# Reordering the first W_up pieces on x1: the third pair's first piece between quarters two and three, the fourth pair in PSUM banks 4 and 5

## The reference, cut to what matters

```python
x = x + rmsnorm(mix, norm_post_mix)                       # x1
hid = jnp.square(jax.nn.relu(rmsnorm(x, norm_pre_mlp) @ w_up))
x = x + rmsnorm(hid @ w_down, norm_post_mlp)              # w_up 2048 x 8192, w_down 8192 x 2048
```

## Time and profile before

| | us |
|---|---|
| median of 3 runs | 1793.79 (1793.65 to 1793.89) |
| the profiled execution | 1794.34 |
| its span, first to last instruction | 1792.7 |
| PE busy | 1775.9 (99%) |
| DVE busy | 1089.4 (61%) |
| ACT busy | 763.9 (43%) |
| POOL busy | 449.3 (25%) |
| granted TensorE clock, mean | 0.999 |

### The profile page before, as it was taken

One profiled execution on the slowest core, in us unless ns is written; L12 is line 12 of the kernel. 1 busy time (PEld: TensorE's weight loads), 2 busy tenths in 40 slices (PEclk: granted clock), 3 DMA queues, 4 the chain that ended last, 5 costly groups with the idle time before them and its releaser, 6 DMA issues.

```text
span 1792.7 us, 34869 instructions
## 1 busy us (share of the span) xinstructions
PE 1775.9 (99%) x13199; PEld 1742.6 (97%) x13199; DVE 1089.4 (61%) x2004; ACT 763.9 (43%) x1116; POOL 449.3 (25%) x351
## 2 busy tenths in 40 slices
PE   8999999999999999999999999999999999999998
PEld 7999999999998989999899999999999999999998
DVE  5587878999778777865875333444344444444444
ACT  7443435555356565633543333333333332333442
POOL 1577776677651222223000000000000000000132
PEclk9999999999999999999999999999999999999999
DMA  8555554554545555554345444544444444454442
GB/s 253 190 177 159 154 155 134 153 153 143 156 150 167 161 181 161 190 192 141 118 145 161 141 152 146 161 152 141 151 138 160 155 147 142 140 158 155 155 142 83
DMA packets 287305, 278.42 MB, mean 155 GB/s; under 512 B 11590, under 2 KB 284718, under 8 KB 286336
## 3 DMA queue, kind: packets, MB, share of 16 engines
q1 hardware_dynamic: 249064, 247.87, 44.0%
q10 hardware_dynamic: 36496, 21.77, 4.1%
q0 software_dynamic: 1648, 7.43, 1.3%
HBM read 261.25 MB, written 17.22 MB: 155 GB/s over the span
## 4 chain that ended last, share of the span: by engine, by line
PE 96%; DVE 2%; ACT 1%; DMA 0%; issue 0%; SPq 0%; DVEq 0%; ACTq 0%
PE ps L1801 29%; PE ps L1803 29%; PE ps L1802 29%; PE ps L2095 1%; PE ps L2045 1%; PE ps L2068 1%; PE ps L2105 1%; PE ps L2139 1%; PE ps L1859 1%; PE ps L2141 1%; PE ps L2140 1%; PE ps L1860 1%; PE ps L1861 1%; DMA xn<-in_x_prompt 0%; DVE mix L1668 0%; DVE wlo L1198 0%
## 5 line engine op out<-in xcount | busy, mean ns | idle before, releaser
L1801 PE MATMUL ps<-ahi,whi 128*128 128x320 f32 x2304 | 717.9, 312 | 0.0
L1803 PE MATMUL ps<-ahi,wlo 128*128 128x320 f32 x2304 | 711.9, 309 | 0.0
L1802 PE MATMUL ps<-alo,whi 128*128 128x320 f32 x2304 | 711.9, 309 | 0.0
L681 ACT ACTIVATE whi<-raw 128x1024 fp32r<-128x1024 f32 x463 | 478.4, 1055 | 446.7 <-PE ps L1803 383.0
L1198 DVE TENSOR_TENSOR wlo<-raw,whi 128x1024 fp32r<-128x1024 f32 x344 | 424.3, 1257 | 236.6 <-ACT whi L681 233.7
L1801 PEld LDWEIGHTS ps<-ahi,whi 128*128 128x128 f32 x2304 | 432.5, 188 | 2.1 <-issue 0.5
L1802 PEld LDWEIGHTS ps<-alo,whi 128*128 128x128 f32 x2304 | 432.6, 188 | 0.5
L1803 PEld LDWEIGHTS ps<-ahi,wlo 128*128 128x128 f32 x2304 | 432.5, 188 | 0.0
L1801 PE MATMUL ps<-hhi,whi 128*128 128x320 f32 x1016 | 314.3, 309 | 0.0
L1803 PE MATMUL ps<-hhi,wlo 128*128 128x320 f32 x1016 | 313.9, 309 | 0.0
L1802 PE MATMUL ps<-hlo,whi 128*128 128x320 f32 x1016 | 313.9, 309 | 0.0
(11 more groups left out here) (324 smaller groups left out, 1603.6 us busy)
## 6 DMA issues: line engine op xcount, KB each, us to landing
raw<-in_w_in SPq DMA_DIRECT2D x144, 512.0 KB, 3.5
raw<-in_w_up SPq DMA_DIRECT2D x128, 512.0 KB, 4.2
raw<-in_w_down SPq DMA_DIRECT2D x128, 512.0 KB, 4.5
raw<-in_w_out SPq DMA_DIRECT2D x64, 512.0 KB, 3.7
h<-in_state_ssm ACTq DMA_DIRECT2D x16, 512.0 KB, 4.9
out<-hout ACTq DMA_DIRECT2D x16, 512.0 KB, 3.2
x_transposed<-xt ACTq DMA_DIRECT2D x1, 2560.0 KB, 13.5
xr<-x_transposed POOLq DMA_DIRECT2D x1, 2560.0 KB, 9.6
```

Source lines behind the costliest of these rows:

```text
L681: act.activation(whi[:, kq, :, 0:width], raw[:, kq, :, 0:width], ACT.Copy).then_inc(hi_done, 1)
L1801: pe.matmul(out, wh, hi[:, kk, :], start=(kk == 0), stop=False)
L1802: pe.matmul(out, wh, lo[:, kk, :], start=False, stop=False)
L1803: last = pe.matmul(out, wl, hi[:, kk, :], start=False, stop=(kk == NT - 1))
```

## The change

The eight pieces of the first two pairs and the four of the third get one written order, `WU_FIRST`, of (pair, quarter): the third pair's first piece stands between the second and the third quarter of the first two pairs. SP loads in this order and then the fourth pair by itself; its loop begins one step later. ACT and DVE do one more split inside the loop over x1 tiles (after t = 12 and t = 13), one of DVE's comes a tile earlier (t = 10 for 11), and the split between DVE's additions is gone. PE runs the third pair's second piece ahead of `rms_x1`. Behind that, DVE does two splits between `qq` and the reciprocal instead of one. The fourth pair goes to banks 4 and 5 and waits for `var2_done` in place of the second `rh`; three `hidden` are written out ahead of the loop of `up`.

```diff
--- before.py
+++ after.py
@@ -66,6 +66,9 @@
 
 
 WS_FIRST = ((0, 0), (0, 1), (1, 0), (1, 1), (0, 2), (1, 2), (0, 3), (1, 3))
+
+
+WU_FIRST = ((0, 0), (1, 0), (0, 1), (1, 1), (2, 0), (0, 2), (1, 2), (0, 3), (1, 3), (2, 1), (2, 2), (2, 3))
 
 
 OUT_BANKS, COL_BANKS = (4, 5, 6, 0, 1, 2, 3), (7, 0, 1)
@@ -386,8 +389,7 @@
                              ).then_inc(raw_ready[s % 4], 16)
             with sp.Fori(1, 4) as i:
                 body(ssd_k, Q_WS, (512 * i, 512 * i + 256), i)
-            for s in range(8):
-                kq, p = s // 2, s % 2
+            for s, (p, kq) in enumerate(WU_FIRST):
                 sp.wait_ge(lo_done[s % 4], Q_MLP + s // 4)
                 sp.dma_start(raw[:, s % 4, :, :], up_k[:, 4 * kq:4 * kq + 4, ds(256 * p, 256)]
                              ).then_inc(raw_ready[s % 4], 16)
@@ -402,7 +404,9 @@
                             load(down_k[:, q, 4 * kq:4 * kq + 4, ds(512 * i + 256 * p, 256)],
                                  q_down(q) + 2 * i + p, kq)
 
-            ups(0, 1)
+            for kq in range(4):
+                load(up_k[:, 4 * kq:4 * kq + 4, 768:1024], Q_MLP + 3, kq)
+            ups(0, 2)
             downs(0)
             with sp.Fori(1, 4) as q:
                 ups(q, 0)
@@ -1086,8 +1090,8 @@
                                ).then_inc(ahi_done, 1)
                 if t % 4 == 3:
                     square_x1(t // 4)
-                if t in (5, 6, 9, 10):
-                    ahead(Q_MLP, 0, {5: 2, 6: 3, 9: 4, 10: 5}[t])
+                if t in (5, 6, 9, 10, 12):
+                    ahead(Q_MLP, 0, {5: 2, 6: 3, 9: 4, 10: 5, 12: 6}[t])
 
 
             act.wait_ge(hout_out, 16 * NT)
@@ -1140,14 +1144,15 @@
                         act.activation(ya[:, ds(4 * i + 2 * p, 2), :], gemm_bank(p), ACT.Copy
                                        ).then_inc(read_act, 1)
 
-            for c in range(6, 10):
+            for c in range(7, 11):
                 ahead(Q_MLP, 0, c)
             act.wait_ge(var2_done, 1)
             act.activation(rb2[:], qq[:], ACT.Sqrt).then_inc(rooted, 1)
-            ahead(q_up(0), 1, 2)
             hidden(0, 0, 0)
+            ahead(q_up(0), 1, 3)
             hidden(0, 0, 1)
-            up(0, 1, c0=3)
+            hidden(0, 1, 0)
+            up(0, 1, c0=4)
             with act.Fori(2, 4) as i:
                 up(0, i)
             with act.Fori(0, 4) as i:
@@ -1679,16 +1684,14 @@
                 x1_part(t)
                 x1_sum(t)
                 x1_lo(t - 1)
-                if t in (4, 7, 8, 11, 12):
-                    ahead(Q_MLP, 0, {4: 1, 7: 2, 8: 3, 11: 4, 12: 5}[t])
+                if t in (4, 7, 8, 10, 12, 13):
+                    ahead(Q_MLP, 0, {4: 1, 7: 2, 8: 3, 10: 4, 12: 5, 13: 6}[t])
             x1_lo(NT - 1)
             for g in range(1, 4):
                 dve.wait_ge(sqx_done, g + 1)
                 if g > 1:
                     dve.wait_ge(dve_step, v)
                 v = st.inc(dve.tensor_tensor(sqx[:, 0:4, :], sqx[:, 0:4, :], sqx[:, 4 * g:4 * g + 4, :], ALU.add))
-                if g == 1:
-                    ahead(Q_MLP, 0, 6)
             dve.wait_ge(dve_step, v)
             dve.sem_inc(acc_done, 1)
             for c in range(7, 9):
@@ -1698,7 +1701,8 @@
             dve.wait_ge(rms_mm, 2)
             dve.scalar_tensor_tensor(out=qq[:], in0=qq[:], scalar=EPS, in1=ps[:, 5, 0:TOK], op0=ALU.mult,
                                      op1=ALU.add).then_inc(var2_done, 1)
-            ahead(Q_MLP, 0, 9)
+            for c in range(9, 11):
+                ahead(Q_MLP, 0, c)
             dve.wait_ge(rooted, 8)
             dve.reciprocal(rb2[:], rb2[:]).then_inc(rms_done, 1)
             dve.wait_ge(rms_done, 1)
@@ -1720,14 +1724,14 @@
                 dve.tensor_tensor(m, m, q1[:].unsqueeze(1).to_broadcast([P, 4, TOK]), ALU.mult
                                   ).then_inc(x1_done, 4)
 
-            def up(q, i, bank0=0, c0=0, x1_from=None):
+            def up(q, i, bank1=2, c0=0, x1_from=None):
                 for c in range(c0, 8):
                     ahead(q_up(q), i, c)
                     if x1_from is not None and c in (1, 5):
                         rescale(x1_from + c // 4)
                     if c % 4 == 3:
                         p = c // 4
-                        hidden(q, i, p, 2 if p else bank0, 4 * (q_up(q) + 2 * i + p) + 4)
+                        hidden(q, i, p, bank1 if p else 0, 4 * (q_up(q) + 2 * i + p) + 4)
 
             def down(q, i, last=False):
                 for c in range(8):
@@ -1750,10 +1754,11 @@
                         m = ya[:, ds(4 * i + 2 * p, 2), :]
                         dve.tensor_tensor(m, gemm_bank(p), m, ALU.add).then_inc(read_dve, 1)
 
-            hidden(0, 0, 0, 0, 4 * Q_MLP + 7)
-            ahead(q_up(0), 1, 2)
-            hidden(0, 0, 1, 2, 4 * Q_MLP + 8)
-            up(0, 1, bank0=6, c0=3)
+            hidden(0, 0, 0, 0, 4 * Q_MLP + 8)
+            ahead(q_up(0), 1, 3)
+            hidden(0, 0, 1, 2, 4 * Q_MLP + 9)
+            hidden(0, 1, 0, 6, 4 * Q_MLP + 12)
+            up(0, 1, bank1=4, c0=4)
             v = st.inc(dve.reciprocal(q1[:], q1[:]))
             dve.wait_ge(dve_step, v)
             up(0, 2, x1_from=0)
@@ -2199,14 +2204,14 @@
 
             pe.wait_ge(read_dve, 16)
             for kq in range(4):
-                for p in range(2):
-                    slot = 2 * (kq % 2) + p
-                    pe.wait_ge(lo_done[slot], Q_MLP + kq // 2 + 1)
+                own = [WU_FIRST.index((p, kq)) for p in range(2)]
+                for n in own:
+                    pe.wait_ge(lo_done[n % 4], Q_MLP + n // 4 + 1)
                 for k in range(4):
                     kk = 4 * kq + k
                     pe.wait_ge(act_ready, 2 * NT + kk + 1)
                     for p in range(2):
-                        slot = 2 * (kq % 2) + p
+                        slot = own[p] % 4
                         for n in range(2):
                             wh, wl = whi[:, slot, k, n * P:(n + 1) * P], wlo[:, slot, k, n * P:(n + 1) * P]
                             out = ps[:, 2 * p + n, 0:TOK]
@@ -2215,13 +2220,15 @@
                             last = pe.matmul(out, wl, ahi[:, kk, :], start=False, stop=(kk == NT - 1))
                         if k == 3:
                             last.then_inc(weights_used, 1)
+                if kq == 1:
+                    piece(4 * Q_MLP + 4, 0, 0, 6, ahi, alo)
+            piece(4 * Q_MLP + 9, 1, 1, 6, ahi, alo)
+            rms_x1()
+            piece(4 * Q_MLP + 10, 2, 2, 6, ahi, alo)
+            piece(4 * Q_MLP + 11, 3, 3, 6, ahi, alo)
+            pe.wait_ge(var2_done, 1)
             for kq in range(4):
-                if kq == 1:
-                    rms_x1()
-                granule(Q_MLP + 2, kq, 6, ahi, alo)
-            pe.wait_ge(rh_done, 2)
-            for kq in range(4):
-                granule(Q_MLP + 3, kq, 2, ahi, alo)
+                granule(Q_MLP + 3, kq, 4, ahi, alo)
             with pe.Fori(2, 4) as i:
                 gemm(q_up(0), i, ahi, alo, lambda p: [(rh_done, 2 * i + p - 1)])
             gemm(q_down(0), 0, hhi, hlo, lambda p: [(rh_done, 7 + p)], (hid_ready, 0, 2))
```

## The result

The changed kernel takes 1800.36 us, median of 7 (1798.50 to 1800.75), against 1793.93 (1793.65 to 1794.40) for the kernel before: a ratio of 1.0034, 95% interval 1.0024 to 1.0044. That is **6.4 us slower**. The forecast was 3.6 us slower, with a range that ended at 1799.6. The profiled execution took 1800.35 us with a span of 1798.7.

A forecast was written before the change was run, and what follows sets the result against it. PE bounds the kernel (busy 1775.9 of 1792.7 us), DVE bounds quarters 2 and 3. Gaining 1.93, losing 2.08, then waiting 3.36 put s14 +3.60 later: 1793.79 + 3.60 = 1797.4 us, range 1796.2 to 1799.6.

The forecast's parts named there:

- the 1.93 us: PE's idle time in quarters 2 and 3 of the first two pairs, which the new order could fill.
- s4: The third pair's first piece, moved between the quarters; to run on PE from 882.27 to 885.79.
- Part 1: Filler piece between the quarters and one more split in the x1 loop: last two quarters run without wait, gain 1.93 us.
- s6: Second piece of the last two quarters; its split ready at 885.67, wanted at 885.79: in time, barely.
- Part 2: Behind the last quarters PE waits for s9's split: 2.08 us lost for 1.93 gained, PE 0.15 later than before.
- s9: The third pair's second piece; PE asks at 899.87, its split lets PE restart at 901.88.
- Part 3: Statistics chain starts a piece later and delays s14's split: a second PE wait of 3.36 us.
- s14: The fourth pair's third piece; wanted by PE at 921.72, got at 925.08, started at 925.15 against 921.55.
- The sum without the clock: s14 starts at 925.15 against 921.55, +3.60 us, and nothing behind it gives this back.
- rival A: Clock falls in the wait for s14: 14 slow matmuls cost 1.7 us more, 1799.1 us; chance 0.33.
- B: Only the wait for s9 appears, s14 does not hang on the chain: 1793.9 us; chance 0.13.
- C: Faster: the filler keeps its 1.93 us, no wait for s9 at 899.87: 1791.9 us; chance 0.04.

The follow-up runs named there:

- both splits early and s12 in the gap: Changed kernel with s9's split between DVE's additions, s14's and s15's before the third hidden, s12's between first rh and first hlo: 1792.08 us, ratio 0.9990.
- second wait filled: Changed kernel with 14 matmuls that nobody reads put ahead of s14, none ahead of s9: 1797.21 us, ratio 1.0022.
- s9 early: Changed kernel with DVE's split of s9 between the first and second addition instead of behind the third: 1796.77 us, ratio 1.0015.
- first wait filled: Changed kernel with 7 matmuls that nobody reads put ahead of s9, none ahead of s14: 1798.79 us, ratio 1.0028.
- s14 early: Changed kernel with the splits of s14 and s15 ahead of the third hidden, on ACT and DVE: 1794.50 us, and 1795.85 us when run again.
- both early: Changed kernel with s9's split between DVE's additions and the splits of s14 and s15 ahead of the third hidden: 1792.37 us, ratio 0.9991.
- both waits filled: Changed kernel with 7 unread matmuls of 512 columns ahead of s9 and 14 ahead of s14: 1797.16 us, ratio 1.0017.
- second wait filled and s9 early: Changed kernel with s9's split between the first and second addition, and 14 unread matmuls ahead of s14: 1795.24 us, ratio 1.0007.

## Why the prediction was wrong

The direction was right and so was every wait. What failed is the size, and it failed in one term.

**What bounds the kernel, and the 1.93 us.** Right: s4 fills them. PE ends the last two quarters 17.60 us after 882.15, which is 120 pitches and no idle time. The kernel with both splits early and s12 in the gap keeps 1.94.

**Part 1.** Right, including the closest fit, s6, where 0.1 us was in hand: its split ended at 885.41, and PE took it up at 885.67 without a wait.

**Part 2.** Right: DVE's additions end and s9's split begins at 900.41, forecast 900.52 with the stage 0.11 earlier; PE's first matmul behind it is at 901.69, forecast 901.88. The piece then took 5.15 us (901.69 to 906.84), forecast 3.59. That is the clock's first fall.

**Part 3.** Right as a chain. In the kernel with the second wait filled, which had no fall when profiled, the first three `rh` came at 912.67, 917.17 and 920.30; forecast 912.75, 917.23 and 920.37. In the changed kernel all of them are 1.5 us later because `rms_x1` was. The wait for s14 was 3.13 us in the records; the fall had moved the piece ahead of it as much as the chain, so it did not shrink.

**The sum without the clock.** 3.60 forecast, 3.51 and 3.52 in the stage of the two kernels that had no fall, 3.1 to 3.2 in their times.

**The clock, the step that failed.** In the sum the clock stands at nothing, for both waits. The prediction set the wait for s14 alone against its two rows, 1.58 us without a fall and 2.2 with one, and made a fall there rival A, with a third of the chance. It never asked the same of the wait for s9, whose forecast 2.0 us (899.87 to 901.88) lie between those rows, so that a fall there has no term, no rival and no chance. Measured: **a stop of 1.94 us (1.77 in the record) brings the clock down in some executions** (by their times 2, 5 and 8 of eleven in three runs), and costs 1.5; the stop of 3.3 to 3.4 us does in at least seven of eleven with s9 early and in all nine with the first wait filled, and costs 1.3 to 1.5, at times 2.7. The price for one fall (1.7 from 14 slow matmuls) was near, since ten to twelve are slow. Both profiled executions of the changed kernel had two falls, 3.6 + 1.5 + 1.3 = 6.4, and the range should have gone up to that. (A single long fall comes near it too, 1799.9 to 1800.1 with the first wait filled, so the times alone do not tell how often each case comes.) The Trainium skill, "TensorE: Matmul & The Clock Gate", in the section on HAM oscillation, describes a kernel that waits between groups of matmuls and is throttled anew at every wait, so that the price is paid each time; the waits of its example are 3 to 5 us long. Here 1.94 us sufficed in some executions, so the measurement goes further than the page. Otherwise this trace agrees: two waits, two falls, 1.3 to 1.5 us each. The prediction had drawn on the first part of that page but applied it to one of two waits.

**The rivals.** A was right in its mechanism and too small by a whole fall. B (only the wait for s9) is what the kernel with s14 early is: +0.4 without a fall and +1.9 with one. C needed both splits in time; that is the kernel with both early, 1.6 below before, and with s12 in the gap 1.9 below, where C put it.

**The chances.** "Same" had 0.39, because the forecast lay on the line of 0.2%. More than half of that rested on the no-fall case, and 0.34% was measured. The chances are also added a little loosely: "slower" counts 0.02 of the 0.03 for something unnamed, and the other half of the forecast, B and C make 0.40 to 0.41.

## What to carry to other kernels

When an engine at full load gets filler work put in front of a wait, go on to the next instructions of the engine that feeds it: here a piece won 1.9 us on PE, and splits that stood too late on DVE took back 5.5. Moving three splits on DVE and two on ACT, with no other change, turned 6 us of loss into 1.6 of gain; a fourth on DVE made it 1.9. And reckon each stop of PE that is near 2 us at its length, and with a chance of about 1.5 us more for slow matmuls behind it, unless unread matmuls fill it; measure such a kernel often, since the fall comes in some executions only.

## What the runs showed of the hardware

- A stop of 1.94 us between dense matmuls sufficed for a fall from 2.4 to 1.2 GHz, and PE was at work again when it came: in the changed kernel about 0.4 us behind the restart (901.69 to 902.06), in the same program again 1.0 us behind it (901.71 to about 902.7), and in s14 early 1.0 (901.50 to about 902.5). So matmuls at full pace just behind a stop do not show that the clock held. By their times, 2 of 11 executions of one program had the fall in one set and 8 of 11 in another, on another chip.
- In one profile with the first wait filled the clock stayed at 0.50 until 930.9, 6 us behind the restart at 924.90, and the stage took 2.7 us longer instead of 1.3.
- The stop near 9 us, 1.58 us long and without a fall in the earlier trace rows, was 2.1 us long in the profile with both waits filled and had one there; the stage began 0.53 later:

```profile
10.00:12.00 2.00, 1.65 (x8) 1.25 (x9) 1.09 (x3) 1.88 (x4) 0.73 (x1) 0.63 1.04 349
12.00:14.00 2.00, 2.00 (x10) 1.48 (x9) 1.03 (x3) 1.80 (x4) 1.18 (x2) 0.52 1.10 347
```

- Seven unread matmuls of 512 columns took 1.77 us in a wait of 1.9 and the clock stayed at 1.00, at no cost in time (3.51 in the stage, against 3.52 without them and without a fall); in eleven executions of the kernel with the second wait filled and s9 early, all lay within 0.32 us.
